# Recurrence's gates: the four blocks of a chunk each in its own quarter of the array, the second gate's halves exchanged back by ScalarE

## What is computed

```python
xc = _causal_conv(x_rnn, conv_w[l], conv_b[l])
xb = xc.reshape(B, S, RNN_BLOCKS, RNN_BLOCK_W)               # 16 blocks of 64
r = jax.nn.sigmoid(jnp.einsum('bshi,hij->bshj', xb, w_rg).reshape(B, S, D_RNN) + b_rg)
i = jax.nn.sigmoid(jnp.einsum('bshi,hij->bshj', xb, w_ig).reshape(B, S, D_RNN) + b_ig)
log_a = -LRU_C * r.astype(jnp.float32) * jax.nn.softplus(-lam.astype(jnp.float32))
a = jnp.exp(log_a)
mult = jnp.sqrt(-jnp.expm1(2.0 * log_a))
bterm = mult * (i * xc).astype(jnp.float32)
_, h = lax.associative_scan(combine, (a, bterm), axis=1)     # h[t] = a[t] h[t-1] + bterm[t]
```

## Time and profile before

| what | us |
|---|---|
| median of 3 runs | 979.6 |
| lowest and highest of them | 979.06 and 979.81 |
| the profiled execution, its own time | 978.87 |
| span of the profiled execution | 977.0 |
| PE busy in it | 963.7 (99%) |
| DVE busy | 536.8 (55%) |
| ACT busy | 479.0 (49%) |
| chain that ended last: share that is PE | 94% |
| gates on PE (L552), first to last start | 41.0 to 89.4 |

### The profile page before, as it was taken

How to read it: one execution, slowest core, us unless ns; L and a number is a source line. 1 busy time by engine, 2 the same in 40 slices (tenths; PEclk the granted TensorE clock), 3 DMA queues, 4 the chain that set the end, 5 groups by cost and what they waited for, 6 DMA issues and landing times.

```text
span 977.0 us, 13582 instructions
## 1 busy us (share of the span) xinstructions
PE 963.7 (99%) x5469; PEld 737.2 (75%) x5469; DVE 536.8 (55%) x853; ACT 479.0 (49%) x766; POOL 2.1 (0%) x10
## 2 busy tenths in 40 slices
PE   9999999999999999999999999999999999999996
PEld 8878887887889888898889887889874455454442
DVE  5888896675666555645577874676352112112113
ACT  5588655756444444444665856445453222222223
POOL 0000000000000000000000000000000000000000
PEclk9999999999999999999999999999999999999998
DMA  9935565524455555554554734384299999999993
GB/s 304 316 130 173 173 216 172 173 87 174 145 179 204 183 173 173 178 197 159 169 167 154 259 109 150 129 284 154 88 364 319 395 393 394 393 393 395 393 394 149
DMA packets 107268, 223.53 MB, mean 229 GB/s; under 512 B 10185, under 2 KB 15042, under 8 KB 107202
## 3 DMA queue, kind: packets, MB, share of 16 engines
q1 hardware_dynamic: 104752, 219.10, 63.3%
q10 hardware_dynamic: 2450, 3.51, 1.2%
HBM read 221.54 MB, written 1.05 MB: 228 GB/s over the span
## 4 chain that ended last, share of the span: by engine, by line
PE 94%; SPq 2%; DVE 1%; DMA 1%; ACT 1%; issue 0%; ACTq 0%
PE pb L463 21%; PE pb L465 20%; PE pb L464 20%; PE pb L2420 12%; PE pb L2443 6%; PE pb L2395 3%; PE pb L2458 3%; PE pb L532 2%; SPq L431 1%; PE pb L603 1%; PE pb L552 1%; PE pb L672 1%; PE pb L2369 1%; PE pb L586 1%; PE pb L695 1%; DMA raw<-in_w_in 1%
## 5 line engine op out<-in xcount | busy, mean ns | idle before, releaser
L1497 DVE TENSOR_TENSOR wl<-raw,wh 128x2048 fp32r<-128x2048 f32 (+2 forms) x113 | 248.7, 2209 | 98.2 <-ACT wh L956 97.8
L956 ACT ACTIVATE wh<-raw 128x2048 fp32r<-128x2048 f32 (+2 forms) x113 | 207.9, 1848 | 112.1 <-PE pb L465 102.9
L463 PE MATMUL pb<-wh,th 128*128 128x512 f32 (+2 forms) x620 | 247.9, 400 | 0.3 <-DVE wl L1497 0.3
L465 PE MATMUL pb<-wh,tl 128*128 128x512 f32 (+2 forms) x620 | 241.5, 389 | 0.0
L464 PE MATMUL pb<-wl,th 128*128 128x512 f32 (+2 forms) x620 | 241.3, 389 | 0.0
L463 PE MATMUL pb<-th,wh 128*128 128x256 f32 x544 | 156.4, 288 | 0.2 <-DVE wl L1980 0.2
L465 PE MATMUL pb<-th,wl 128*128 128x256 f32 x544 | 153.5, 282 | 0.0
L464 PE MATMUL pb<-tl,wh 128*128 128x256 f32 x544 | 153.2, 282 | 0.0
L463 PEld LDWEIGHTS pb<-wh,th 128*128 128x128 f32 x620 | 116.7, 188 | 27.6 <-issue 4.1
L465 PEld LDWEIGHTS pb<-wh,tl 128*128 128x128 f32 x620 | 116.6, 188 | 25.4
L464 PEld LDWEIGHTS pb<-wl,th 128*128 128x128 f32 x620 | 116.9, 189 | 22.7
(11 more groups left out here) (394 smaller groups left out, 1084.4 us busy)
## 6 DMA issues: line engine op xcount, KB each, us to landing
raw<-in_w_in SPq DMA_DIRECT2D x31, 1024.0 KB, 5.1
raw<-in_w_up SPq DMA_DIRECT2D x16, 1024.0 KB, 5.5
raw<-in_w_down SPq DMA_DIRECT2D x16, 1024.0 KB, 4.8
raw<-in_w_exp_gate SPq DMA_DIRECT2D x20, 512.0 KB, 10.2
raw<-in_w_exp_up SPq DMA_DIRECT2D x20, 512.0 KB, 11.5
raw<-in_w_exp_down SPq DMA_DIRECT2D x10, 1024.0 KB, 14.0
raw<-in_w_xkv SPq DMA_DIRECT2D x8, 1024.0 KB, 5.1
mwh<-in_w_exp_gate SPq DMA_DIRECT2D x14, 512.0 KB, 11.8
```

What stands on the lines that cost most here:

```text
L463: PE.matmul(o, lh, rh, start=start, stop=False, skip_group_check=True)
L465: return PE.matmul(o, ll, rh, start=False, stop=stop, skip_group_check=True)
L956: ACTE.activation(hi_of(i), raw_of(i), ACT.Copy).then_inc(S["hi"], 1)
L1497: DVE.tensor_tensor(lo_of(i), raw_of(i), hi_of(i).bitcast(F), ALU.subtract).then_inc(S["lo"], 1)
```

## The change

`pe_rnn_gates` sends the i gate's (j = 1) two products to the other half of the array's columns: half h of `XC` is multiplied into the PSUM partitions of half 1-h. So each of a chunk's four 64x64 blocks stands in a quarter of the array of its own: rows of half h, columns of half h for r, of half 1-h for i. The i gate gets its own bank (b + 2, that is 2 or 3) instead of the second half of bank b. Since its halves are swapped in PSUM, ScalarE reads them in two activations of 64 partitions by 256, each from the other half's partitions, and writes them to the right ones in `T2`. `gate_a` counts 6 to a chunk instead of 5, and all waits on it follow. `pe_turn_k`, which writes banks 2 and 3, waits for the i gate of chunk 7 to be read. The loops, the sizes of the matmuls and their number stay.

```diff
--- before.py
+++ after.py
@@ -540,22 +540,24 @@
             m.then_inc(S["row_mm"], 1)
 
         def pe_rnn_gates(c):
+
             b, xc = c % 2, XC[c % 2]
             PE.wait_ge(S["xc"], c + 1)
             if c == 0:
                 PE.wait_ge(S["d_bd"], 64)
             if c >= 2:
-                PE.wait_ge(S["gate_a"], 5 * (c - 2) + 2)
+                PE.wait_ge(S["gate_a"], 6 * (c - 2) + 3)
             for j in range(2):
                 for h in range(2):
-                    ps = slice(64 * h, 64 * h + 64)
-                    m = PE.matmul(PB[b][ps, 256 * j:256 * j + 256], BDv[j][ps, c, :], xc[ps, :], start=True, stop=True,
+                    ps, o = slice(64 * h, 64 * h + 64), 64 * (h ^ j)
+                    m = PE.matmul(PB[b + 2 * j][o:o + 64, 0:256], BDv[j][ps, c, :], xc[ps, :], start=True, stop=True,
                                   skip_group_check=True)
             m.then_inc(S["gate_mm"], 1)
 
         def pe_turn_k():
 
             PE.wait_ge(S["rope"], 8)
+            PE.wait_ge(S["gate_a"], 6 * 7 + 3)
             for j in range(2):
                 for c in range(2):
                     for t in range(2):
@@ -1012,13 +1014,15 @@
             ACTE.activation(T1, PB[b][:, 0:256], ACT.Tanh, bias=hb[:, c:c + 1], scale=0.5).then_inc(S["gate_a"], 1)
             if c >= 1:
                 ACTE.wait_ge(S["rnn_u"], c)
-            ACTE.activation(T2, PB[b][:, 256:512], ACT.Tanh, bias=hb[:, 8 + c:9 + c], scale=0.5).then_inc(S["gate_a"], 1)
-            ACTE.wait_ge(S["gate_a"], 5 * c + 1)
+            for h in range(2):
+                ps, o = slice(64 * h, 64 * h + 64), slice(64 - 64 * h, 128 - 64 * h)
+                ACTE.activation(T2[ps, :], PB[b + 2][o, 0:256], ACT.Tanh, bias=hb[ps, 8 + c:9 + c], scale=0.5).then_inc(S["gate_a"], 1)
+            ACTE.wait_ge(S["gate_a"], 6 * c + 1)
             if c == 0:
                 ACTE.wait_ge(S["square"], 4)
             for dst, k in ((S1, sp4n), (S0, sp8n)):
                 ACTE.activation(chunk(dst, c), T1, ACT.Exp, bias=k[:, c:c + 1], scale=k[:, c:c + 1]).then_inc(S["gate_a"], 1)
-            ACTE.wait_ge(S["gate_a"], 5 * c + 4)
+            ACTE.wait_ge(S["gate_a"], 6 * c + 5)
             ACTE.activation(T1, T1, ACT.Tanh, bias=sp4[:, c:c + 1], scale=sp4[:, c:c + 1]).then_inc(S["gate_a"], 1)
 
         def act_root():
@@ -1585,13 +1589,13 @@
 
         def dve_rnn_in(c):
 
-            DVE.wait_ge(S["gate_a"], 5 * c + 2)
+            DVE.wait_ge(S["gate_a"], 6 * c + 3)
             DVE.wait_ge(S["xc"], c + 1)
             DVE.scalar_tensor_tensor(XR[:, c, 0:256], T2, 1.0, XC[c % 2], ALU.add, ALU.mult).then_inc(S["rnn_u"], 1)
 
         def dve_rnn_mult(c):
             mm = chunk(S0, c)
-            DVE.wait_ge(S["gate_a"], 5 * c + 5)
+            DVE.wait_ge(S["gate_a"], 6 * c + 6)
             DVE.scalar_tensor_tensor(mm, mm, 1.0, rnn_t1(c), ALU.add, ALU.mult).then_inc(S["rnn_m"], 1)
 
         def dve_gelu_in(j):
```

## The result

| | before | changed |
|---|---|---|
| median of 8 runs, us | 979.78 | 980.92 |
| lowest | 979.06 | 980.35 |
| profiled execution, its own time | 978.87 | 981.08 |
| its span | 977.0 | 979.2 |

The ratio is 1.0019, 95% interval 1.0010 to 1.0028: the change costs 1.9 us (1.0 to 2.7), where 0.4 was forecast. The ratio is taken over all runs; the medians alone are 1.1 us apart, because some runs of the changed kernel are much longer than its median (up to 984.62). Its median lies 0.9 us above the forecast of 980.0, inside the stated range (978.5 to 982.0) and on the side that was forecast.

The account below looks back on a forecast made before the run. The ScalarE-VectorE chain, handing PE its low halves, was taken to bound the kernel: 1.08 us later, it moves unit 18 from 124.38 to 124.77, whatever PE gains. So 979.6 + 0.4 = 980.0 us, range 978.5 to 982.0.

Parts of the forecast that it names:

- What bounds the kernel: From 38 to 130 us, the ScalarE-VectorE chain sets its own pace and hands PE weights; least ahead at unit 18.
- PE's gates: Chunks' gate matmuls on PE: four pairs become two groups of four, saving 0.47 us a chunk, 3.7 us of PE's list.
- the case in which pairs stay: Rival at PE's gates: quarters still run in pairs, PE's list stays, time still 980.0; 7%.
- the one in which they shut each other out: Rival at PE's gates: products run one behind the other, 7.5 us more in all, 987.1; 5%.
- ScalarE's gates: One activation more per chunk on ScalarE, each half costing 0.36 us start to start, 2.9 us in all.
- The places: Where ScalarE's addition lands: chunks 0, 1, 3, 5, 7 hidden; 2, 4, 6 on the path, 0.36 each, 1.08 us.
- The sum at unit 18: Low half there at 123.69 + 1.08 = 124.77, PE started at 124.38 before: 0.4 us later, whatever its gates gain.
- The range: Kernel time from 978.5 to 982.0 us, from ScalarE's cost bounds 978.9 and 981.8 with some tenths for spread.
- eight additions of 0.36 on the path: Rival at ScalarE's gates: all additions on the path, or each dearer than a pipelined row; +2.2, 981.8 us; 10%.
- The prediction's own signs: Trace checks: ScalarE's reads 0.36 apart, low half at 121.40 1.1 later, PE waiting 3 to 4 us, later rows 0.4 later.
- The new wait for k: `pe_turn_k` waiting on chunk 7's gate costs nothing, since it stands four units behind chunk 7's gates.
- The slack of 0.69 us: At unit 18 the low half is there at 123.69, PE begins at 124.38; PE's gain beyond this becomes a wait.

Follow-up runs that it names:

- the kernel with two reads alone: Kernel before with only ScalarE's part: gate i read in two activations of 64 partitions, PE's gates as before; ratio 1.0023, median 981.75 us.
- PE's part alone: Changed kernel with gate i read in one activation of 128 partitions, its halves left exchanged; ratio 1.0005 to before, median 979.24 us.
- the count over seven kernels: One trace each of before and six variants: low half of unit 18's arrival (-1.7 to +3.3 us) against first gate to last matmul (-1.3 to +3.5).
- the last three kernels: Moves bringing low halves earlier against PE (room), in the changed kernel, the one before, and PE's part with one read: ratios 0.9979, 0.9995, 0.9967.
- the one with the bank of its own: Kernel before with gate i's products in bank b + 2 but the same quarters as gate r's, one read; one execution, 980.07 us.

## Why the prediction was right or wrong

- **What bounds the kernel** was read rightly: not PE's list but the low halves of units 17 and 18. Shown by the kernel with two reads alone (as slow as the whole change), by PE's part alone (no gain near 3.4), by the count over seven kernels and by the last three kernels (with room, the gain arrives).
- **PE's gates**: 0.47 us a chunk forecast, 0.42 measured: the first of the three steps is 0.27 us and stays, the two that go are 0.21 to 0.22 each. All four quarters run together; the case in which pairs stay and the one in which they shut each other out fell.
- **ScalarE's gates** is the term that was mis-sized. "The start-to-start time of such a row is ... 0.35 and ... 0.36" was taken over from rows of one first partition to rows that change it. The row that I used for halving, 96 partitions against 128, is right about the duration (0.47 for 64 partitions against 0.46) and says nothing on overlap. Measured 0.76 a chunk, more than PE's 0.42 and not less.
- **The places** held. Chunk 2 added 0.74 (1.02 - 0.28), chunk 4 0.78 (1.80 - 1.02), chunk 6 0.77 (2.57 - 1.80). Chunk 1, forecast as just hidden with 0.42 of room for 0.36, passed 0.28 on: 0.76 - 0.42 = 0.34, a little less measured. 0, 3, 5 and 7 were hidden. Sum 2.56 instead of 1.08.
- **The sum at unit 18**: 2.56 - 0.69 = 1.87, and 0.1 for the restart that I left out, where the trace has 2.0 and the ratio 1.9 (1.0 to 2.7). With the right price the same sum gives the measured time.
- **The range held by luck.** Its upper bound, 981.8, was drawn for eight additions of 0.36 on the path. That did not happen: three and part of a fourth came through, at twice the price. The same rival also named "or each costs more than a pipelined row"; this half of it is what happened, but it had no price of its own, and the rival was given 10%.
- **The prediction's own signs** speak against it. It was to be wrong if the low half at 121.40 moved by 2 us or more, and that moved by 2.56. The two reads were to stand 0.36 apart and stand 0.50 apart; rows behind 130 us were to be 0.4 later and are 2.1 to 2.2 later; PE was to wait 3 to 4 us and gave up 5.4.
- **The new wait for k** cost nothing by itself, but `pe_turn_k` waited 1.5 us for VectorE's rotary embedding, as forecast, hidden in what was lost anyway.
- **The slack of 0.69 us** is that of one execution. The start of the gates against the other two engines' chain differs by about 1 us either way between profiled executions (in the profile of two reads alone PE was 0.3 later and the chain 0.6 earlier than in that of before, in the one with the bank of its own 0.8 and 1.8 later), so the slack and the loss do too, as the count over seven kernels shows. How it is spread over the unprofiled runs is not known.

## What to carry to other kernels

An engine that is busy 99% of the time may still be one whose list can't be shortened for profit: find the place where its suppliers are closest behind it, and price a change by what it does to the supplier there. Price an added instruction by its start-to-start time between the neighbours that it will have, not by that of the row that it replaces. Two engines that show no wait for each other can be exactly balanced, as at unit 9 here, and then a step put on one of them comes out whole.

## What the runs showed of the hardware

- ScalarE: of two neighbouring activations of which the second did not wait for the first's result, the second started about 0.1 us before the first's end when both began at partition 0 on the reading and on the writing side, with 64 or 128 partitions, in one bank or two. Where the first partition changed there was a gap of 0.025 us instead: 0.12 us for each change (256 columns, from PSUM).
- ScalarE, not explained: in the kernels that cut gate i by partitions and wrote each half where it was read, the instruction behind a high half of 128 by 2048 also came with the gap of 0.025 us, though both began at partition 0. With the halves crossed, in the changed kernel, it overlapped.
- TensorE: four plain fp32 matmuls of 64 by 64 by 256, each in its own quarter of the array, ran together, with starts 7 ns apart; two of them at a time write one bank in different partitions. The eight records of a chunk took 0.66 us instead of 1.08.
- TensorE: on units of 512 columns, the first matmul behind a wait for weights was followed by the next after 0.34 us instead of 0.23. The first behind the gates was too, with no wait.
